# One layer of a 1-core transformer kernel: the expert loop written out, the usual branch first, and the one-hot gather and return as rounded products

## The reference

```python
def moe_swiglu(h, w_router, b_router, w_gate, w_up, w_down):
    logits = (h @ w_router).astype(F32) + b_router.astype(F32)
    top_logits, top_idx = lax.top_k(logits, TOP_K)
    top_w = jax.nn.softmax(top_logits, axis=-1)
    gates = jnp.sum(jax.nn.one_hot(top_idx, N_EXPERTS, dtype=F32) * top_w[..., None], axis=-2)
    out = jnp.zeros(h.shape, F32)
    for e in range(N_EXPERTS):
        y_e = swiglu(h, w_gate[e], w_up[e], w_down[e]).astype(F32)
        out = out + gates[..., e:e + 1] * y_e
    return out.astype(h.dtype)
```

## Time and profile before

| | |
|---|---|
| median of 3 runs | 2756.8 us (2753.82 to 2760.43) |
| the profiled execution's own time | 2760.41 us |
| its span, first to last instruction | 2758.6 us |
| mean granted TensorE clock | 0.957 |
| PE busy | 2595.6 us, 94% |
| DVE busy | 1915.8 us, 69% |
| ACT busy | 1484.0 us, 54% |
| expert layer, first gather to the next layer's first product | 952.99 to 1992.86 us of the span |

### The profile page before, as it was taken

The page is one execution under the profiler, slowest core; times in us unless marked ns, Lnnn a source line. Parts: engine busy times, 40 slices in busy tenths (PEclk is TensorE's granted clock), DMA queues, the critical chain, the costliest instruction groups (busy, mean ns, idle before and its releaser), DMA issues.

```text
span 2758.6 us, 40927 instructions
## 1 busy us (share of the span) xinstructions
PE 2595.6 (94%) x16009; PEld 2299.6 (83%) x16009; DVE 1915.8 (69%) x2422; ACT 1484.0 (54%) x1798; POOL 183.8 (7%) x200
## 2 busy tenths in 40 slices
PE   6998989999889899999999999999899999898998
PEld 6766989999789788888788878787797899887998
DVE  6885366544756497979797888888774675565773
ACT  3222365435554376767576767676635564435653
POOL 0000012212010100000000000000000121100120
PEclk9988999999999899999999999999997999988998
DMA  7221044554324299989899999999751355351550
GB/s 216 89 100 46 1 154 142 183 184 153 123 77 138 81 384 352 350 319 369 297 364 325 360 326 357 322 363 349 263 186 62 122 184 174 96 190 47 169 184 31
DMA packets 339196, 567.81 MB, mean 206 GB/s; under 512 B 17592, under 2 KB 184869, under 8 KB 338885
## 3 DMA queue, kind: packets, MB, share of 16 engines
q1 hardware_dynamic: 326394, 556.47, 57.9%
q10 hardware_dynamic: 12618, 8.72, 1.1%
HBM read 564.10 MB, written 2.24 MB: 205 GB/s over the span
## 4 chain that ended last, share of the span: by engine, by line
PE 85%; DVE 7%; ACT 5%; issue 2%; ACTq 1%; POOL 0%; DMA 0%; DVEq 0%; POOLq 0%
PE bank L205 22%; PE bank L207 22%; PE bank L206 22%; PE bank L2039 4%; ACT chunks_hi L317 2%; DVE chunks_lo L325 2%; PE bank L1711 1%; PE bank L3129 1%; PE bank L3123 1%; PE bank L1728 1%; PE bank L3144 1%; PE bank L2585 1%; PE bank L2572 1%; PE bank L2586 1%; PE bank L2091 1%
## 5 line engine op out<-in xcount | busy, mean ns | idle before, releaser
L3253 DVE TENSOR_TENSOR weight_lo<-ring,weight_hi 128x2048 fp32r<-128x2048 f32 x336 | 765.6, 2290 | 159.4 <-ACT weight_hi L3202 157.5
L3202 ACT ACTIVATE weight_hi<-ring 128x2048 fp32r<-128x2048 f32 x336 | 643.5, 1918 | 260.6 <-PE bank L207 257.0
L325 DVE TENSOR_TENSOR chunks_lo<-ring,chunks_hi 128x2048 fp32r<-128x2048 f32 x175 | 403.3, 2305 | 303.7 <-ACT chunks_hi L317 303.5
L205 PE MATMUL bank<-x_parts,chunks_hi 128*128 128x256 f32 x1568 | 454.8, 290 | 22.1 <-DVE x_parts L408 13.3
L317 ACT ACTIVATE chunks_hi<-ring 128x2048 fp32r<-128x2048 f32 x175 | 333.7, 1908 | 245.5 <-PE bank L207 240.7
L206 PE MATMUL bank<-x_parts,chunks_hi 128*128 128x256 f32 x1568 | 447.5, 285 | 0.0
L207 PE MATMUL bank<-x_parts,chunks_lo 128*128 128x256 f32 x1568 | 447.3, 285 | 0.0
L205 PE MATMUL bank<-weight_hi,xg_parts 128*128 128x512 f32 x896 | 358.4, 400 | 5.9 <-DVE weight_lo L3253 4.3
L207 PE MATMUL bank<-weight_hi,xg_parts 128*128 128x512 f32 x896 | 350.9, 392 | 0.0
L206 PE MATMUL bank<-weight_lo,xg_parts 128*128 128x512 f32 x896 | 350.5, 391 | 0.0
L205 PEld LDWEIGHTS bank<-x_parts,chunks_hi 128*128 128x128 f32 x1568 | 304.2, 194 | 28.5 <-issue 17.2
(11 more groups left out here) (518 smaller groups left out, 4727.6 us busy)
## 6 DMA issues: line engine op xcount, KB each, us to landing
ring<-in_moe_w_gate SPq DMA_DIRECT2D x112, 1024.0 KB, 6.2
ring<-in_moe_w_up SPq DMA_DIRECT2D x112, 1024.0 KB, 6.3
ring<-in_moe_w_down SPq DMA_DIRECT2D x112, 1024.0 KB, 7.0
ring<-in_w_up SPq DMA_DIRECT2D x44, 1024.0 KB, 5.1
ring<-in_w_in SPq DMA_DIRECT2D x24, 1024.0 KB, 5.3
ring<-in_w_down SPq DMA_DIRECT2D x22, 1024.0 KB, 4.9
ring<-in_xa_w_kv SPq DMA_DIRECT2D x16, 1024.0 KB, 5.5
ring<-in_da_w_qkv SPq DMA_DIRECT2D x12, 1024.0 KB, 5.1
```

The source lines that it names most:

```text
L205: pe.matmul(dst, l[0], r[0], start=first, stop=False, skip_group_check=True)
L325: dve.tensor_tensor(self.lo[:, n % SPLITS], ring[:, c.slot], self.hi[:, n % SPLITS].bitcast(F32), ALU.subtract).then_inc(self.rest.sem, se ...
L3202: act.activation(weight_hi[:, slot(m, odd + next_)], ring[:, m % RING], ACT.Copy)\
L3253: dve.tensor_tensor(weight_lo[:, at_], ring[:, m % RING], weight_hi[:, at_].bitcast(F32), ALU.subtract)\
```

## The change

- The eight experts are written out; the hardware loops on PE, ACT, DVE and SP go. SP waits for `weights_lo` before each chunk.
- The usual path is in the `If`, the slow path in the `Else`.
- The tokens are kept as two rounded parts (`xt_parts`), without the root. `gather` makes 32 rounded matmuls of 128 columns, high parts into banks 0 and 1, low parts into banks 2 and 3, and two float32 matmuls of 2 columns that bring each slot's root and gate (`choice` to `share`). The root goes in as the scale of Silu, gate times root as the scalar of the up product. The matrix `to_token` goes; the transposed `to_slot` serves the return.
- y is split into two rounded parts. ACT copies the high part (now after `upper`), `leave` on PE subtracts it from the product in banks 4 and 5 (two matmuls of 512 columns), ACT copies the rest (`rest_of_y`). `to_tokens` makes 16 rounded matmuls of 256 columns into banks 6, 7, 4 and 5, all behind the first block, and DVE adds at m = 4 and 5.
- In the prelude PE turns the tokens before the router's products; ACT copies them before the root, DVE takes the rest. A DMA of the next layer's bias moves from the prelude to `enter` on ACT's queue.

The diff, cut to what the text speaks of:

```diff
@@ -1244,6 +1245,9 @@
                     carry_square(act, n)
                 for c in range(1, SPLITS):
                     weights.upper(act, first_chunk + c)
+                act.wait_ge(sig("bias_boarded").sem, 32)
+                act.dma_start(memn[:, 0:6], bass.AP(board_rows.tensor, P - 1, [[6 * 384 - 1, P], [384, 6], [1, T]]))\
+                   .then_inc(sig("bias_boarded").sem, sig("bias_boarded").tick(16))
...
-                pe.wait_ge(consts_in.sem, consts_in.total)
-                pe.matmul(bank[6][:, 0:E], ones[0:1, :], row_b[0:1, :], start=True, stop=True)
-                for t in range(TT):
-                    for k in range(DT):
-                        if t == 0:
-                            pe.wait_ge(*ready(k))
-                        mm = pe.matmul(bank[4 + t][:, 0:E], x[:, k, t * P:(t + 1) * P], wr[:, k], start=k == 0,
-                                       stop=k == DT - 1)
-                    mm.then_inc(routed.sem, routed.tick())
-                sum_x(pe, full=False, rows=True)
+                pe.wait_ge(*ready(DT - 1))
                 for n in range(4):
                     t, half = divmod(n, 2)
                     for m in range(4):
                         mm = pe.transpose(bank[n][:, m * P:(m + 1) * P], x[:, 4 * half + m, t * P:(t + 1) * P], ident[:])
                     mm.then_inc(turned.sem, turned.tick())
+                pe.wait_ge(consts_in.sem, consts_in.total)
+                pe.matmul(bank[6][:, 0:E], ones[0:1, :], row_b[0:1, :], start=True, stop=True)
+                for t in range(TT):
+                    for k in range(DT):
+                        mm = pe.matmul(bank[4 + t][:, 0:E], x[:, k, t * P:(t + 1) * P], wr[:, k], start=k == 0,
+                                       stop=k == DT - 1)
+                    mm.then_inc(routed.sem, routed.tick())
+                sum_x(pe, full=False, rows=True)
                 pe.wait_ge(chosen.sem, chosen.at(1))
-                pe.wait_ge(copied.sem, copied.at(4))
+                pe.wait_ge(rested.sem, rested.at(4))
...
-                act.wait_ge(sig("bias_boarded").sem, 32)
-                act.dma_start(memn[:, 0:6], bass.AP(board_rows.tensor, P - 1, [[6 * 384 - 1, P], [384, 6], [1, T]]))\
-                   .then_inc(sig("bias_boarded").sem, sig("bias_boarded").tick(16))
-                root_x(act, full=False, rows=True)
-                act.wait_ge(x_rooted.sem, x_rooted.at(1))
                 for n in range(4):
                     t, half = divmod(n, 2)
                     act.wait_ge(turned.sem, turned.at(n + 1))
-                    act.activation(xt[:, t, half * 512:(half + 1) * 512], bank[n][:, :], ACT.Copy,
-                                   scale=x_col[:, 2 * t:2 * t + 1])\
+                    act.activation(xt_parts[0][:, t, half * 512:(half + 1) * 512], bank[n][:, :], ACT.Copy)\
                        .then_inc(copied.sem, copied.tick())
+                root_x(act, full=False, rows=True)
...
+                dve.tensor_scalar(minus[:], ident[:], -1.0, None, ALU.mult)
+                for n in range(4):
+                    t, half = divmod(n, 2)
+                    c_ = slice(half * 512, (half + 1) * 512)
+                    dve.wait_ge(copied.sem, copied.at(n + 1))
+                    dve.tensor_tensor(xt_parts[1][:, t, c_], bank[n][:, :], xt_parts[0][:, t, c_].bitcast(F32), ALU.subtract)\
+                       .then_inc(rested.sem, rested.tick())
...
-                body(0, 0, True, False)
-                with eng.Fori(0, (E - 2) // 2) as pair:
-                    body(pair * 2 + 1, 1, False, False)
-                    body(pair * 2 + 2, 0, False, False)
-                body(E - 1, 1, False, True)
+                for e in range(E):
+                    body(e, e % 2, e == 0, e == E - 1)
 
...
-                    i_ = dve.tensor_scalar(to_token[:, t], to_slot[:, t], gates_[:, t, bass.ds(e + ahead, 1)], None,
+                    i_ = dve.tensor_scalar(choice[:, t, 0:1], ones[:, 0:1], scaled_gates[:, t, bass.ds(e + ahead, 1)], None,
...
             def gather(pe):
-                for half in range(2):
-                    for q in range(4):
-                        m = 4 * half + q
-                        for t in range(TT):
-                            mm = pe.matmul(bank[half][:, q * P:(q + 1) * P], xt[:, t, m * P:(m + 1) * P], to_slot[:, t, 0:P],
-                                           start=t == 0, stop=t == TT - 1)
-                    mm.then_inc(gathered.sem, 4)
+
+                for t in range(TT):
+                    pe.matmul(bank[7][:, 0:2], to_slot[:, t, 0:P].bitcast(F32), choice[:, t], start=t == 0, stop=t == TT - 1)
+                for c_ in range(2):
+                    for half in range(2):
+                        for q in range(4):
+                            m = 4 * half + q
+                            for t in range(TT):
+                                mm = pe.matmul(bank[2 * c_ + half][:, q * P:(q + 1) * P], xt_parts[c_][:, t, m * P:(m + 1) * P],
+                                               to_slot[:, t, 0:P], start=t == 0, stop=t == TT - 1)
+                        mm.then_inc(gathered.sem, 1)
 
             def to_tokens(pe, b, dst):
                 for q in range(2):
-                    mm = pe.matmul(dst[:, q * T:(q + 1) * T], ye[:, 0, (2 * b + q) * P:(2 * b + q + 1) * P], gt[:, 0],
-                                   start=True, stop=True)
+                    for c_ in range(2):
+                        mm = pe.matmul(dst[:, q * T:(q + 1) * T], ye_parts[:, c_, (2 * b + q) * P:(2 * b + q + 1) * P],
+                                       from_slot[:], start=c_ == 0, stop=c_ == 1)
                 mm.then_inc(back.sem, 1)
+
+            def leave(pe, e):
+
+                for half in range(2):
+                    wait(pe, y_out, e, half + 1)
+                    pe.matmul(bank[4 + half][:, :], minus[:], ye_parts[:, 0, half * 512:(half + 1) * 512], start=False,
+                              stop=True, skip_group_check=True).then_inc(y_left.sem, 1)
...
-                    wait(pe, tokens_lo, e, 8)
+                    wait(pe, tokens_lo, e, 2)
+                    wait(pe, fetched, e, 3)
...
-                            if b == 0 and not first:
-                                wait(pe, y_out, e, 0)
-                                for g_ in range(2 * which, 2 * which + 2):
-                                    if g_ >= 2:
-                                        wait(pe, added, e, g_ - 5)
-                                    to_tokens(pe, g_, bank[6 + g_ % 2][:, :])
+                            if b == 0 and which == 0 and not first:
+                                leave(pe, e - 1)
+                        if b == 0 and not first:
+                            wait(pe, y_rest, e - 1, 2)
+                            for g_ in range(4):
+                                to_tokens(pe, g_, bank[(6, 7, 4, 5)[g_]][:, :])
...
+                            wait(pe, acts_lo, e, NB - 1)
                             gather(pe)
 
                 experts(pe, body)
-                wait(pe, y_out, E, 0)
+                leave(pe, E - 1)
+                wait(pe, y_rest, E - 1, 2)
...
+                def rest_of_y(e):
+                    for half in range(2):
+                        wait(act, y_left, e, half + 1)
+                        act.activation(ye_parts[:, 1, half * 512:(half + 1) * 512], bank[4 + half][:, :], ACT.Copy)\
+                           .then_inc(y_rest.sem, 1)
...
+                            if b == 0:
+                                wait(act, fetched, e, 3)
+                            act.activation(sg[:, b % 2], bank[2 * b % 4][:, :], ACT.Silu, scale=share[:, 1:2])\
+                               .then_inc(gated.sem, 1)
+                        if m == 2 and not first:
+                            rest_of_y(e - 1)
                         if m + AHEAD < NC:
                             upper(e, m + AHEAD, odd)
                         elif not last:
                             upper(e, m + AHEAD - NC, odd, 1)
+                        if m == NC - 1:
+                            for half in range(2):
+                                act.activation(ye_parts[:, 0, half * 512:(half + 1) * 512], bank[4 + half][:, :], ACT.Copy)\
+                                   .then_inc(y_out.sem, 1)
...
-                        dve.tensor_tensor(xg_parts[:, 1, fs], bank[half][:, :].rearrange("p (a b) -> p a b", b=P),
-                                          xg_parts[:, 0, fs].bitcast(F32), ALU.subtract).then_inc(tokens_lo.sem, 4)
+                        wait(dve, gathered, e, half + 3)
+                        dve.tensor_copy(xg_parts[:, 1, 4 * half:4 * half + 4],
+                                        bank[2 + half][:, :].rearrange("p (a b) -> p a b", b=P)).then_inc(tokens_lo.sem, 1)
...
+                            dve.scalar_tensor_tensor(out=prod[:, b % 2], in0=bank[(2 * b + 1) % 4][:, :], scalar=share[:, 0:1],
```

(20 more changed lines are left out.)

126 lines of the change are left out of this document (64 added, 62 removed).

## The result

| | before | after |
|---|---|---|
| median | 2758.61 us (2753.82 to 2763.22, 4 runs) | 2720.61 us (2719.48 to 2721.84, 4 runs) |
| ratio after / before | | 0.9862, 95% interval 0.9844 to 0.9881 |
| profiled execution | 2760.41 us | 2719.68 us |
| span, mean granted clock | 2758.6 us, 0.957 | 2717.7 us, 0.964 |

The change makes the kernel 38.0 us faster (32.8 to 43.0 by the interval). It took 1992.86 - 929.25 = 1063.6 us and takes 1955.53 - 924.97 = 1030.6: **33.0 us of the profiles' 40.9 lie in it**; 4.3 are ahead of it and 3.6 behind it, in code that the change leaves alone.

The account below looks back on a forecast made before the run. PE's stream was taken as the bound, DMA close behind. Terms summing to -32.2 us took the profiled 2760.4 to 2728.2; the median's 3.6 us offset gave 2724.6 us, range 2716 to 2731, chance 57%.

Parts of the forecast that it names:

- The return: Seven returns inside the expert stream: PE's wait for DVE goes and rounded passes replace float32 ones, -24.2 us.
- Clock: Behind three of the seven return gaps: no gap means no fall of PE's granted clock, -5.0 us.
- The loop's turns: PE's two branches back in the expert loop: both gaps and a clock fall go once written out, -6.1 us.
- The gather: Seven gathers inside the stream: 32 rounded matmuls at 0.12 us plus `choice` cost more than before, +5.5 us.
- The start: Layer's start after the fence: no jump over the slow path, so the gather begins earlier, -3.4 us.
- The prelude: Transposes before the router: effect depends on PE's granted clock, taken as 0, bounds -4.7 and +1 us.
- The end: Layer's end: the jump now stands there, partly offset by the shorter return, +1.0 us.
- Short gather: Gather: columns limit the matmuls, 0.067 us each, 12 us less, giving 2712 us; chance 14%.
- Long gather: Gather: matmuls cost 0.215 us each, 24 us more, giving 2749 us; chance 10%.
- The new wait: Return: ACT copies the rest of y too late and PE waits 16.6 us in all, giving 2741 us; chance 6%.
- the turns are DVE's: Gaps where the expert loop turns come from DVE and stay, giving 2731 us; chance 5%.
- Instructions: PE's straight stream through eight experts: instruction fetches stall PE, 75 us if each does, giving 2800 us; chance 5%.

Follow-up runs that it names:

- four_banks: Kernel before, with the return's parts 2 and 3 sent to banks 4 and 5, still in float32; median 2732.28 us, layer 1039.6 us.
- f32_return: Changed kernel with the return in float32, without `leave` and ACT's copy of the rest of y; median 2731.93 us, layer 1037.6 us.
- rest_late: Changed kernel with ACT's copy of the rest of y moved behind the `upper` of the same turn; median 2728.20 us, layer 1034.4 us.
- branch: Kernel before with only the three If/Else pairs swapped, usual path in the If; median 2764.90 us, layer 1073.0 us.
- narrow_gather: Changed kernel with the gather's rounded matmuls cut from 128 to 64 columns; median 2733.77 us, layer 1039.5 us.
- after_again: Changed kernel run again, unedited; median 2722.12 us, layer 1031.2 us.
- line_pe: Kernel before with PE's stream alone written out for all eight experts; median 2752.87 us, layer 1059.4 us.
- line_all: Kernel before with PE, ACT, DVE and SP all written out, SP waiting before each chunk; median 2752.75 us, layer 1062.4 us.
- warm_last: Changed kernel with 9, 2 and 3 idle PE matmuls before the choice wait, behind the counting of places, behind the fence; median 2726.81 us, layer 1031.0 us.
- warm_short: Changed kernel with 9, 8 and 5 idle PE matmuls before the choice wait, behind the counting of places, behind the fence; median 2719.60 us, layer 1027.7 us.

## Why the prediction was right, point by point

The time came out 4.0 us below the forecast, inside its own range (2716 to 2731). The bounds that the prediction names for that range, the prelude's and the end's, give only 2718.9 to 2727.9; the time lies in these too. The layer itself gave 33.0 us for a sum of 32.2, so the rest is mostly the code around it: together its two stretches took 1695.0 us in before's profile and 1687.1 in after's, where the other twelve average 1690.6 (1688.0 to 1694.4). The first was a long one by 4.4 us, for which the prediction took 3.6 off, the second a short one by 3.5, which it could not know. That the layer's sum came out so close is luck in part: the start is 4.7 us worse than its term, and the gather, the prelude and the end are 2.2, 1.9 and 0.8 better.

- **The return, -24.2: -23.9.** The gap is 2.38 (2.35 to 2.59 in four_banks), the passes with `leave` 1.03 (f32_return), x 7. The cover for ACT's copies was put at 1.5 us and is 1.4 (rest_late).
- **Clock, -5.0: -5.0.** "If no gap means no fall" held in four_banks and after. In before three experts of seven had it, in variants with the same gaps four and five.
- **The loop's turns, -6.1: -6.3**, from 131.69 + 130.71 + 129.26 less 3 x 127.35 and two falls (127.35 is 124.97 + 2.38; with the mean of the two quiet experts, 127.44, it is 6.0). PE's own, as argued against the rows' releaser. But the price is no constant: 2.6 us in four_banks, 10.4 in branch.
- **The gather, +5.5: about +3.3.** The sum's mis-sized term. 0.12 was taken for a rounded matmul of 128 columns and 0.114 measured, `choice` 0.36 for 0.44: by the rows 0.5 a gather for 0.8; by the ladder of experts 0.42 (four_banks 124.97, f32_return 125.39). That columns are not the limit narrow_gather shows; that the operand's load is, stays the likely reason and is not shown by itself. The Trainium skill, TensorE: Matmul & The Clock Gate, section Back-to-back issue gap, with its 81 ns for 128 columns, does not agree with the trace's 114 for these operands.
- **The start, -3.4: +1.3.** The failed step. The jump went, as said (3.15 in branch). "`choice` (half clock) 0.9, gather 3.84 and 1.5 for three microseconds at half clock, as before" did not hold: the whole gather and the first dozen products ran at 0.50. From places to first product 952.99 - 939.86 = 13.13 for 959.73 - 946.00 = 13.73, so -0.6; and expert 0, 2.4 us longer with 0.5 of that its gather, gives 1.9 back. The counting of places ran at half clock as well, so the gather starts 4.41 us behind it where the prediction had 3.5.
- **The prelude, 0: -1.9.** From the last `o_parts` product to the places 14.89 for 16.75, inside the bounds -4.7 to +1. The transposes kept half clock and the router got the full one.
- **The end, +1.0: +0.2, and +0.7 in after_again.** The prediction let the end follow PE. It follows DVE's last addition, 6.09 us behind the last product before and after, so that PE is done 0.4 us earlier (5.00 for 5.37) bought nothing. ACT went on 0.31 us behind that addition before, and in branch too, whose jump stands there and was free. With the short return it goes on 0.52 (after) or 1.05 us (after_again) behind it, released by PE's sequencer, and in all five profiles that have this return at full clock 1.8 us behind the end of a q8 packet. So the jump cost 0.2 to 0.7, under the 1.8 to 2.6 that the term took.
- These make -23.9 - 5.0 - 6.3 + 3.3 + 1.3 - 1.9 + 0.2 = -32.3, for 33.0 measured.
- **The rivals.** Short gather: no, 0.114. Long gather: no. The new wait: no; it appears once, 0.7 us, at the layer's end, where nothing covers it. That the turns are DVE's: no (line_pe). Instructions: no stall in the straight stream of after, nor in line_all. The mechanism exists, though: branch shows it at 3.6 to 4.1 us a time behind taken branches, each time with an instruction packet under way.

## What to carry to other kernels

Where PE's stream is the bound, read its starts in order of time: a wait costs its length and sometimes a clock fall behind it, and the fall comes behind some of the same gaps and not behind others, so take the gap out rather than price the fall. Judge a reordering of branches and the removal of a loop as one: the first alone was slower here because the loop's code moved. A gap with no releaser, or with one that makes no sense, can be held against the times of the instruction packets. And check which of two clocks the trace grants where an engine comes out of a fence before adding up matmuls there.

## What was not expected

- **A second stall behind a taken branch**, 3.6 and 4.1 us, five products after the branch, only because other code had moved (branch).
- **A clock fall without idle time**: 32 matmuls of 64 columns, 0.112 us apart, were followed by a clock of 0.5 in four of the seven experts, those of 128 columns at 0.114 in none of seven profiles.
- **A clock of 0.50 for 21 us** with PE busy 19.87 of them (warm_last), while in warm_short it rose at about 950.4, some 9 us after the first idle matmul. Between the two lie six more idle matmuls behind the places and two behind the fence. What decides there stays open.
- **The spread.** Before's 29 runs reach over 17.6 us (2749.03 to 2766.60), the change's two sets of four over 2.4 and 2.3. Four runs reach less far than 29 in any case, and kernels whose profile has no fall in the stream are not all so even: four_banks' six runs reach over 10.2 us, rest_late's five over 6.3. What sets the spread is not settled.
